# One level of Strassen's method for the up and down projections of a ConvFFN in a hybrid decoder layer

## The reference

```python
def conv_ffn(x, w_up, w_ffn_conv, b_ffn_conv, w_down):
    hid = jnp.einsum('bsd,df->bsf', x, w_up)          # 2048 -> 2 x 5632
    hid = causal_dwconv(hid, w_ffn_conv, b_ffn_conv)  # width 3, along the positions
    val, gate = hid[..., :D_FF], hid[..., D_FF:]
    return jnp.einsum('bsf,fd->bsd', jax.nn.silu(gate) * val, w_down)

def reference(x, ...):
    mix = hybrid_mixer(x, ...)     # input projection, short conv, mLSTM of 4 heads, output projection
    x = layer_norm(alpha * x + mix, ln1_g, ln1_b)
    return layer_norm(alpha * x + conv_ffn(x, ...), ln2_g, ln2_b)
```

## Time and profile before

| | us |
|---|---|
| three timed runs | 2342.16, 2343.01, 2343.11 |
| median | 2343.01 |
| profiled execution: span from first to last instruction | 2341.3 |
| around the span (median less span) | 1.7 |
| TensorE matmul busy, share of the span | 2302.4 (98%) |
| VectorE busy | 1099.8 (47%) |
| ScalarE busy | 588.2 (25%) |
| GpSimd busy | 103.9 (4%) |

### The profile page before, as it was taken

One profiled execution on the slowest core, in us unless ns is written; L12 is line 12 of the kernel. 1 busy time (PEld: TensorE's weight loads), 2 busy tenths in 40 slices (PEclk: granted clock), 3 DMA queues, 4 the chain that ended last, 5 costly groups with the idle time before them and its releaser, 6 DMA issues.

```text
span 2341.3 us, 24919 instructions
## 1 busy us (share of the span) xinstructions
PE 2302.4 (98%) x10248; PEld 1895.4 (81%) x10248; DVE 1099.8 (47%) x1130; ACT 588.2 (25%) x488; POOL 103.9 (4%) x62
## 2 busy tenths in 40 slices
PE   8999999999999998999999999999999999999996
PEld 7888888888888887888888888888888888888885
DVE  4354324433345569544444444544444444444448
ACT  4323222221133352222221212222221212222221
POOL 0000000000000039000000000000000000000003
PEclk9999999999999999999999999999999999999998
DMA  5322222232336532222222222222222222222231
GB/s 222 108 90 73 92 98 79 90 127 90 107 137 223 193 149 73 107 99 98 90 101 96 90 102 95 90 94 103 90 95 102 90 97 100 90 90 107 90 126 72
DMA packets 37151, 249.55 MB, mean 107 GB/s; under 512 B 4092, under 2 KB 4124, under 8 KB 7920
## 3 DMA queue, kind: packets, MB, share of 16 engines
...
HBM read 244.67 MB, written 4.19 MB: 106 GB/s over the span
## 4 chain that ended last, share of the span: by engine, by line
PE 95%; DVE 3%; DMA 1%; ACT 0%; issue 0%; POOL 0%; SPq 0%; DVEq 0%; ACTq 0%
PE ps L948 32%; PE ps L949 32%; PE ps L950 31%; DVE w_lo L567 1%; DMA raw<-w_mix 1%; DVE stream L886 0%; DVE stream L883 0%; PE ps L1148 0%; ACT w_hi L382 0%; DVE x_full L866 0%; DVE stream L816 0%; PE ps L1006 0%; POOL act_lo L354 0%; PE ps L978 0%; PE ps L977 0%
## 5 line engine op out<-in xcount | busy, mean ns | idle before, releaser
L948 PE MATMUL ps<-act_hi,w_hi 128*128 128x512 f32 (+1 forms) x2080 | 806.5, 388 | 10.0 <-DVE w_lo L567 6.2
L382 ACT ACTIVATE w_hi<-raw 128x2048 fp32r<-128x2048 f32 x220 | 421.8, 1917 | 1527.2 <-PE ps L950 1524.6
L949 PE MATMUL ps<-act_lo,w_hi 128*128 128x512 f32 (+1 forms) x2080 | 804.1, 387 | 0.0
L950 PE MATMUL ps<-act_hi,w_lo 128*128 128x512 f32 (+1 forms) x2080 | 804.0, 387 | 0.0
L567 DVE TENSOR_TENSOR w_lo<-raw,w_hi 128x2048 fp32r<-128x2048 f32 x219 | 512.9, 2342 | 358.3 <-ACT w_hi L382 358.3
L948 PEld LDWEIGHTS ps<-act_hi,w_hi 128*128 128x128 f32 x2080 | 392.1, 189 | 92.3 <-DVE w_lo L567 6.8
L950 PEld LDWEIGHTS ps<-act_hi,w_lo 128*128 128x128 f32 x2080 | 391.9, 188 | 79.1
L949 PEld LDWEIGHTS ps<-act_lo,w_hi 128*128 128x128 f32 x2080 | 392.1, 188 | 78.3
L949 PE MATMUL ps<-w_lo,h_hi 128*128 128x512 f32 x704 | 280.9, 399 | 0.0
L948 PE MATMUL ps<-w_hi,h_hi 128*128 128x512 f32 x704 | 277.4, 394 | 0.0
L950 PE MATMUL ps<-w_hi,h_lo 128*128 128x512 f32 x704 | 275.9, 392 | 0.0
...
## 6 DMA issues: line engine op xcount, KB each, us to landing
...
```

The source lines that it names most:

```text
L382: act.activation(w_hi[:, s % SPLIT, :], raw[:, s % RAW, :], ACT.Copy).then_inc(tile_hi, 1)
L948: pe.matmul(dst, a[0], b[0], start=first, stop=False)
L949: pe.matmul(dst, a[0], b[1], start=False, stop=False)
L950: return pe.matmul(dst, a[1], b[0], start=False, stop=last)
```

## The change

**The method.** Strassen's method (in Winograd's form) multiplies two matrices, each cut in 2 by 2 blocks, with 7 block products for 8, and pays with sums of blocks. For the up projection a *unit* is one tile of values and one of gates. Its weights are cut by value and gate and by the two halves of the 2048 inputs; the activations by the same halves and by the two halves of the 512 positions. A unit is 7 products of 8 blocks by 3 matmuls of 256 columns. The first pair of tiles stays as it was, in the window, and 43 units follow. For the down projection the 44 hidden tiles are taken in pairs, in 6 chunks (five of 4 pairs, one of 2); for each of the 7 products a pair is one *slot* of 12 matmuls of 512 columns.

**Sums.** The four weight sums of an up unit (128x1024 each) are done by POOL (`s1`, `s3`, `s2`, `s4` in this order), as are those of each down pair, except the four first sums of the first down chunk, which DVE does. The four activation sums of the up projection (128x2048) are done once by DVE; those of the down projection by POOL, four of 128x1024 for each chunk of 4 pairs. In place of 2048 the parts are 1024 wide: ACT and DVE make a high and a low part for each of the 7 products, from sums where the product needs one, into 3 buffers for up (two products ahead) and 5 for down (four ahead).

**Results.** Products are summed in PSUM where they can be; ACT copies four 128x256 results of a unit to SBUF (`hid`) and DVE adds the three others (`hid_add`). The first tap of the convolution is done by ACT, the two later ones by DVE, now from SBUF (`later_taps`). The finished hidden tile goes to DRAM (`h_dram`) and comes back in chunks, to be split there. The normalised rows go to DRAM too; POOL makes the scaled residual from them in 8 pieces of 128x1024, in units 4, 6, ... 18, and it comes back into `acc` before the down projection. The FFN part is written out instead of looped.

```diff
+ORDER = ("P1", "P2", "P6", "P5", "P7", "P3", "P4")
+NP = len(ORDER)
+N_UP = NP * GROUPS
+AHEAD = 2
+CHUNK_PAIRS = [4, 4, 4, 4, 4, 2]
+DOWN_SLOTS, DOWN_AHEAD = 5, 4
+BLOCK = {"P1": A11, "P2": A12, "P6": A11, "P5": AX, "P7": A21, "P3": AX, "P4": A22}
+TARGET = {"P1": (0, 0), "P2": (0, 0), "P6": (1, 0), "P5": (1, 1), "P7": (1, 1), "P3": (1, 0), "P4": (0, 1)}
...
+    def load_unit(m):
+        if m == 1:
+            sp.wait_ge(tile_lo, FF0 + 2)
+        elif m == 2:
+            sp.wait_ge(tile_done, FF0 + 2)
+        else:
+            sp.wait_ge(up_lo, NP * (m - 2))
+        sp.dma_start(unit[m % 2][:, A11:A12 + 1, :],
+                     w_up[2 * m].rearrange("p (b n) -> p b n", b=2)).then_inc(val_in[m % 2], 16)
+    def store_hidden(t):
+        sp.wait_ge(prod_ready, t + 1)
+        sp.dma_start(h_dram[t], prod[t % 2][:, :]).then_inc(h_out[t % 2], 16)
...
+    for m in range(1, GROUPS - 1):
+        store_hidden(m - 1)
+        load_unit(m + 2)
+        if m >= 3 and m % 2 and (m - 3) // 2 < PIECES:
+            load_residual((m - 3) // 2)
+        if m >= 4 and m % 2 == 0 and (m - 4) // 2 < PIECES:
+            store_residual((m - 4) // 2)
...
-    pool.wait_ge(x1_turned, KD)
-    pool.wait_ge(pool_step, 1)
-    for c in range(NS):
-        pool.tensor_tensor(rows[:, c, :], rows[:, c, :], ln_rows[:, 0, :], ALU.mult).then_inc(pool_step, 1)
-        pool.wait_ge(pool_step, c + 2)
-        pool.tensor_tensor(rows[:, c, :], rows[:, c, :], ln_rows[:, 1, :], ALU.add).then_inc(res_ready, 1)
+    for m in range(1, GROUPS + 1):
+        u = unit[m % 2]
+        pool.wait_ge(gate_in[m % 2], 16 * (loads_before(m) + 1))
+        pool.tensor_tensor(u[:, AX, :], u[:, A21, :], u[:, A22, :], ALU.add).then_inc(s1_up, 1)
+        pool.wait_ge(s1_up, m)
+        pool.wait_ge(val_in[m % 2], 16 * (loads_before(m) + 1))
+        pool.tensor_tensor(u[:, A21, :], u[:, A11, :], u[:, A21, :], ALU.subtract).then_inc(s3_up, 1)
+        pool.wait_ge(s3_up, m)
+        pool.wait_ge(up_lo, NP * (m - 1) + 1)
+        pool.tensor_tensor(u[:, A11, :], u[:, AX, :], u[:, A11, :], ALU.subtract).then_inc(s2_up, 1)
+        pool.wait_ge(s2_up, m)
+        pool.wait_ge(up_lo, NP * (m - 1) + 4)
+        pool.tensor_tensor(u[:, AX, :], u[:, A12, :], u[:, A11, :], ALU.subtract).then_inc(s4_up, 1)
+        r = (m - 4) // 2
+        if m >= 4 and m % 2 == 0 and r < PIECES:
+            if r % NS == 0:
+                pool.wait_ge(res_gb_in, 32 * (r // NS + 1))
+                pool.tensor_scalar(res_gb[:, :, :], res_gb[:, :, :], ALPHA, None, ALU.mult).then_inc(res_scaled, 1)
+                pool.wait_ge(res_scaled, r // NS + 1)
+            pool.wait_ge(res_z_in, 16 * (r + 1))
+            pool.tensor_tensor(res_z[:, :], res_z[:, :], res_gb[:, 0, :], ALU.mult).then_inc(res_mult, 1)
+            pool.wait_ge(res_mult, r + 1)
...
+    def down_s1(c, p):
+        n = sum(CHUNK_PAIRS[:c]) + p
+        if p == 0:
+            pool.wait_ge(da_in[A21], 16 * (c + 1))
+            pool.wait_ge(da22_in[c % 2], 16 * (c // 2 + 1))
+            pool.wait_ge(down_lo, SLOT0[c] - CHUNK_PAIRS[c - 1])
+        pool.tensor_tensor(dx[:, p, :], da21[:, p, :], da22[c % 2][:, p, :], ALU.add).then_inc(s1_down, 1)
...
+            for p in range(g):
+                down_s1(c, p)
+            for p in range(g):
+                down_s3(c, p)
+            down_t1(c, g)
+            down_t2(c, g)
+            for p in range(g):
+                down_s2(c, p)
+            down_t3(c, g)
+        for p in range(g):
+            down_s4(c, p)
+        down_t4(c, g)
+    pool.wait_ge(ln2_in, 32)
+    for f, c in enumerate(FIN):
...
+    def up_split(n):
+        m, i = unit_of(n)
+        if n >= 3:
+            act.wait_ge(up_done, n - 2)
+        else:
+            act.wait_ge(tile_done, FF0 + 2) if n else act.wait_ge(tile_lo, FF0 + 2)
+        if ORDER[i] in ("P1", "P2"):
+            act.wait_ge(val_in[m % 2], 16 * (loads_before(m) + 1))
+        elif ORDER[i] == "P4":
+            act.wait_ge(gate_in[m % 2], 16 * (loads_before(m) + 1))
+        else:
+            act.wait_ge({"P6": s2_up, "P5": s1_up, "P7": s3_up, "P3": s4_up}[ORDER[i]], m)
+        act.activation(slot_hi[(n + 2) % 3][:, :], unit[m % 2][:, BLOCK[ORDER[i]], :], ACT.Copy).then_inc(up_hi, 1)
...
+    def silu(m):
+        if m:
+            act.wait_ge(up_conv, 4 * m)
+        else:
+            act.wait_ge(ff_step, 6)
+        act.activation(yy[:, 1, :], yy[:, 1, :], ACT.Silu).then_inc(silu_done, 1)
...
+    def up_lo_part(n):
+        m, i = unit_of(n)
+        dve.wait_ge(up_hi, n + 1)
+        dve.tensor_tensor(slot_lo[(n + 2) % 3][:, :], unit[m % 2][:, BLOCK[ORDER[i]], :],
+                          slot_hi[(n + 2) % 3][:, :].bitcast(F32), ALU.subtract).then_inc(up_lo, 1)
...
+    def later_taps(m, t):
+        g = m - 1
+        c = (2 * m + t) * 4
+        dve.wait_ge(tap, 2 * g + t + 1)
+        for lag in (1, 2):
+            if lag == 2:
+                dve.wait_ge(up_conv, 4 * g + 2 * t + 1)
+            dve.scalar_tensor_tensor(yy[:, t, lag:SEQ], hid[g % 2][:, t, 0:SEQ - lag], fc[:, c + 2 - lag:c + 3 - lag],
+                                     yy[:, t, lag:SEQ], ALU.mult, ALU.add).then_inc(up_conv, 1)
...
+    for n in range(N_UP):
+        m, i = unit_of(n)
+        if n and ORDER[(n - 1) % NP] in ("P2", "P7", "P3"):
+            hid_add(n - 1)
+        if n + AHEAD < N_UP:
+            up_lo_part(n + AHEAD)
+        if n == 0:
+            gated(0)
+        if m > 1 and i in (1, 2):
+            later_taps(m - 1, i - 1)
+        if m > 1 and i == 4:
+            gated(m - 1)
...
+        for j in range(8):
+            last = mm3(ps[:, up_bank(m, i), 0:256], (hi[:, P * j:P * j + P], lo[:, P * j:P * j + P]),
+                       (xb[:, i, 0, j, :], xb[:, i, 1, j, :]), fresh and j == 0, j == 7, not fresh)
+        last.then_inc(up_done, 1)
...
+    def down_half(s, u):
+        c, i, p = DOWN[s]
+        what, g, k = ORDER[i], CHUNK_PAIRS[c], NP * c + i
+        fresh = what in ("P1", "P2", "P5") and p == 0
+        h, hi, lo = hc[k % 2], dslot_hi[s % DOWN_SLOTS], dslot_lo[s % DOWN_SLOTS]
+        for q in range(2):
+            last = mm3(ps[:, (0 if k % 2 else 4) + 2 * u + q, :],
+                       (h[:, 0, p, P * u:P * u + P], h[:, 1, p, P * u:P * u + P]),
+                       (hi[:, 512 * q:512 * q + 512], lo[:, 512 * q:512 * q + 512]), fresh, p == g - 1,
+                       what not in ("P1", "P2", "P5"))
+        return last
```

More of the change, by code:

```diff
@@ L63 @@
 FF0 = N_MIX + N_OUT
-GR0 = FF0 + 2
 CONV0 = MIX.index(("conv", 0, 0))
@@ L163, in build @@
[L163 to L173 removed]
+        ident = at("ident", [P, P], SM)
@@ new lines, in _ @@
+            hid_split(0, 0)
+            down_split(0)
+            hid_copy(N_UP - 1)
+            first_tap(GROUPS, 0)
+            first_tap(GROUPS, 1)
+            for s in range(1, DOWN_AHEAD):
+                down_split(s)
+                if s == 1:
+                    silu(GROUPS)
+            for s in range(N_DOWN):
+                c, i, p = DOWN[s]
+                if p == 0:
+                    k = NP * c + i + 1
+                    if k < NP * CHUNKS:
+                        hid_split(k // NP, k % NP)
+                if s + DOWN_AHEAD < N_DOWN:
+                    down_split(s + DOWN_AHEAD)
@@ new lines, in gated @@
+            def gated(m):
+                dve.wait_ge(silu_done, m + 1)
+                if m >= 2:
+                    dve.wait_ge(h_out[m % 2], 16 * (m // 2))
+                if m:
+                    dve.wait_ge(up_conv, 4 * m)
+                dve.tensor_tensor(prod[m % 2][:, :], yy[:, 1, :], yy[:, 0, :], ALU.mult).then_inc(prod_ready, 1)
+            dve.wait_ge(x1_full_act, sum(full_on_act(a) for a in range(2 * KD)))
+            dve.wait_ge(x1_full_dve, sum(not full_on_act(a) for a in range(2 * KD)))
@@ new lines, in down_product @@
+            def down_product(s):
+                c, i, p = DOWN[s]
+                what, g, k = ORDER[i], CHUNK_PAIRS[c], NP * c + i
+                pe.wait_ge(down_lo, s + 1)
+                if p == 0:
+                    pe.wait_ge(hc_lo, k + 1)
+                    if k == 0:
+                        pe.wait_ge(hid_dve, 3 * GROUPS)
+                    elif k == 1:
+                        pe.wait_ge(hid_act, 4 * GROUPS)
+                    else:
+                        pe.wait_ge(added, 2 * (k - 1))
+                for u in range(2):
+                    last = down_half(s, u)
+                last.then_inc(down_done, 1)
@@ new lines, in _ @@
+            for n in range(N_UP):
+                up_product(n)
+            end = N_DOWN - CHUNK_PAIRS[CHUNKS - 1]
+            for s in range(end):
+                down_product(s)
+            k = NP * CHUNKS - 1
+            pe.wait_ge(hc_lo, k + 1)
+            pe.wait_ge(added, 2 * (k - 1))
+            for u in range(2):
+                for s in range(end, N_DOWN):
+                    if u == 0:
+                        pe.wait_ge(down_lo, s + 1)
```

(2 more changed lines are left out.)

750 lines of the change are left out of this document (510 added, 240 removed).

## The result

The changed kernel takes 2510.29 us (median of 4 runs, 2508.93 to 2511.24) against 2343.06 (2342.16 to 2343.12) of the kernel before: a ratio of 1.0714, 95% interval 1.0699 to 1.0729. The forecast was 2567 with a range of 2385 to 2655, and slower with 0.90.

A forecast was written before the change was run, and what follows sets the result against it. The prediction took TensorE's matmul time to bound the kernel before. From 2343 us it added 171 (up), 34 (down), 14 (into the units) and 5 (tail) for 2567 us, range 2385 to 2655.

The forecast's parts named there:

- The mechanism: POOL's operations and DVE's two-input SBUF operations exclude each other and take turns; in up the port needs 21.1 us, TensorE 20.1.
- the signs: Trace marks of a right forecast, among them PE well below 90% busy and low parts of 1024 averaging 2 us or more.
- Rival A: The POOL-DVE lock seldom binds, TensorE stays the bound: about 2229 us, faster; chance 0.08.
- Rival B: The port is packed well, at its sum of 21.1 us per up unit: 2374 us, still slower; chance 0.17.
- Rival C: The clock falls in ordinary up units too, 77 us more from idle times of 1.7 and 2.3 us: 2644 us; chance 0.20.
- into the units: Between window and up units: first activation and weight sums delay the units' effective begin to 905 from 890.5, +14 us.
- The walk from x: One up unit's operations followed from the end of P5's low part: P3 starts at x + 12.55, 24.1 us in all.
- the clock's price: In eight up units with residual work, matmuls slow at granted clock 0.50: 2.2 us more each, 18 us.
- they count in full: In the up phase, the residual's POOL operations push sums and DVE operations behind them, adding their whole length: 48 us.
- costed at nothing: The DRAM round trips: no cost assumed; without cover at the first down chunk, its start gets up to 10 us longer.
- the port's sum: Lower bound of a down chunk of 4 pairs: POOL and DVE port operations add to 88 us, against TensorE's 78.
- The matmul saving: Up matmuls 936 to 865 us, down 493 to 431: together 133 us less, if TensorE never waits.

The follow-up runs named there:

- e2: Changed kernel with POOL's four up sums written to a block no product reads, products reading stored blocks (output differs): 2509.77 us, 1.0711 of the kernel before.
- e3: Changed kernel with the convolution's running sum moved to two free PSUM banks, so later taps and the gated product read PSUM; everything computed: 2365.29 us, 1.0097.
- e4: Changed kernel with POOL's arithmetic on the residual left out, loads and signals kept, so the output lacks the residual: 2460.57 us, 1.0503 of the kernel before.
- e6: e3 with eight of a down chunk's weight sums (the two s1 and s3) made on DVE in place of POOL: 2359.47 us, 1.0069 of the kernel before.
- e10: e3 with the down projection written as eight plain block products without sums, the up projection still by Strassen: 2325.51 us, 0.9928 of the kernel before.
- e12: e10 plus the residual's POOL work placed in the gaps of odd units, a unit later; everything computed: 2310.31 us, 0.9862 of the kernel before.

## Why the prediction was right, and where it was off

**The mechanism** held at every step that the runs could try. TensorE falls to 89%; its waits in the up phase end with `slot_lo` (152.6 of 155.5 us); `hid_add` stayed at 0.41 us; the granted clock dips in the units with residual work. Two of the signs were set too high: TensorE at 89% isn't well below 90%, and the mean low part is 1.71 and 1.95 us where 2 or more was expected. Rival A, that the lock seldom binds, is out: the units are 23.3 us long, and e2 and e3 show that it is POOL's work beside DVE's operations in SBUF that makes them so. Rival B, packed to its sum (21.1 us), lay 2.2 us below the measured unit. Rival C didn't come: from 1400 us on the granted clock is 1.00. But the idle times there, 0.93 and 1.58 us in each unit, are shorter than the 1.7 and 2.3 us that C was built on, so that much idle time in every unit was not tried.

**By terms, in us:**

| step | forecast | measured |
|---|---|---|
| an up unit | 24.2 | 23.3 |
| 43 units | 1041 | 1002 |
| residual and clock in the up phase | 66 | 50 (e4), 51 (trace) |
| up phase against before | +171 | +115 |
| down against before | +34 | +32 |
| into the units | +14 | +11 |
| tail | +5 | +10 |
| sum (of the unrounded rows) | +224 | +167 |

The measured up phase runs from 901.3 us (the start of the second unit, 924.6, less one unit) to 1951.9, so it is 1050.6 us long; that is 3 less than 1002.3 and 51.4, since the last unit takes 20 us.

**The up unit.** The walk from x (1448.00, the end of P5's low part) puts P3 at x + 12.55; its matmul stands at 1459.59, x + 11.6. The order of the operations was right to the last one. (The list of a unit's DVE operations ahead of the prediction also begins here, with P5's low part.) What was mis-sized are the steps at which the two engines take turns. From x on, the first tap and `s4` take 2.9 us (forecast 3.1), the second tap and `s1` 2.8 (3.1), P7's low part and `s3` 3.3 (3.55), the two taps 1.3 (1.55) and P3's low part 1.15: each of the first four is 0.2 to 0.3 shorter than the sum of the free durations. In the rows an operation begins before the one ahead of it has ended, as the tap at 1447.91 and `s4` at 1448.14; but a row also holds the wait for the other engine, so where in a turn the time is saved can't be read from them. The remaining part of the walk, from P3 to the next x, was forecast at 11.65 and is 11.7. This step is 39 of the 57 us by which the sum is too high.

**Residual and clock.** The full count of POOL's operations (48) and the clock's price (18) made 66. The excess over 41 units of 23.31 is 51 us in the trace, and e4 gives 49.7 for both together. No run takes the clock away alone, but the trace of the changed kernel divides the 51 us. Unit 8, which has residual work, and unit 22, which has none, each from its first matmul to the next unit's:

```profile
1076.59:1106.37 29.78, 23.14 (x171) 22.73 (x170) 24.58 (x16) 10.43 (x14) 17.27 (x7) 0.89 0.36 133
1442.27:1465.57 23.30, 20.79 (x171) 20.32 (x170) 20.84 (x16) 10.43 (x14) 11.25 (x5) 1.00 0.26 98
```

Unit 8 is 6.5 us longer. TensorE stands still for 6.6 us in it and for 2.5 in unit 22, so 4.1 us are waits; the other 2.35 are the same 168 matmuls (three more lie across the edges), which take longer at a granted clock of 0.89. Added up over the eight units with a piece, the waits are 33 us and the slower matmuls 18. The clock's price was right in sum (2.3 us a unit, though 1.1 to 4.6 in the single ones). The term that was too high is "they count in full": 48 us of POOL's work made 33 us of waiting.

**Down.** 527 us were forecast and 525 measured (1951.9 to 2476.6), but the agreement is luck: it has two errors in it that cancel. A chunk takes 91.7 us and not 96, and 5.5 of them 504 where 528 stood. The first chunk's faster `s1` and the last one's missing successor were to give 13 back and the start to take 12. Nothing came back at the end: the fifth chunk takes 86.0 us and the last half one 52.1, as much as one and a half of 91.7. And 20 us are lost at the entry: TensorE waits 2.4, 8.9, 1.7 and 7.1 us between 1955 and 2001. POOL had stood waiting 18.7 us for hidden rows on their way back from DRAM before it began these sums, a round trip that was costed at nothing; whether it or the order of DVE's queue is what holds up the entry was not tried. In the steady chunks the waits look like this in the trace of the changed kernel:

```profile
2246.76 0.77 PE L1393 MATMUL ps<-dslot_hi,hc 128*128 128x512 f32 x1 [5.51 <-DVE acc L1320]
```

```profile
2232.08 3.42 DVE L1290 TENSOR_TENSOR dslot_lo<-da22a,dslot_hi 128x1024 fp32r<-128x1024 f32 x1
2235.42 3.42 DVE L1297 TENSOR_TENSOR hc<-hb,hc 128x1024 fp32r<-128x1024 f32 x1
2238.77 3.42 DVE L1290 TENSOR_TENSOR dslot_lo<-da,dslot_hi 128x1024 fp32r<-128x1024 f32 x1
2242.11 1.21 DVE L1320 TENSOR_TENSOR acc<-acc,ps 128x1024 f32<-128x1024 f32 x1
2243.24 2.24 DVE L1290 TENSOR_TENSOR slot_lo<-da,slot_hi 128x1024 fp32r<-128x1024 f32 x1
2245.41 1.21 DVE L1320 TENSOR_TENSOR acc<-acc,ps 128x1024 f32<-128x1024 f32 x1
```

The two accumulations for which TensorE waits, at 2242.11 and 2245.41, read PSUM and take 1.21 us. They are late since three operations ahead of them in DVE's queue take 3.4 us each. The forecast's bound of 88 us (the port's sum) had the right size for another reason: DVE's own 57 us and 32 behind POOL. e6 excluded the sum, and e10 did without both parts.

The forecast priced a lower clock in the up units with residual work and put it at nothing in the down chunks. There it costs more. Of the 91.7 us of a steady chunk (the table under e6) 76.2 are 336 matmuls at 0.2267 and 11.0 are TensorE's four waits; the remaining 4.4 are matmuls that follow more slowly, at a granted clock of 0.94. In e10's chunk, without a wait, the granted clock is 1.00 and nothing remains. Over 5.5 chunks that makes 24 us at most (an estimate from this one chunk: some of it follows each wait at a full clock too, as in unit 22, where TensorE is busy for 20.8 us with matmuls that take 20.16 in e3).

**The tail** took 10 us more than before where one `finish` was put down at 5.

**The matmul saving** was right as a rate. With 0.120 us at 256 columns, e3's units run at 20.16 us, 867 in all for 936 before. It can be had only where nothing else is longer, which is what e12 shows. The Trainium skill's formula ("TensorE: Matmul & The Clock Gate", Back-to-back issue gap), which the page gives for an isolated matmul at full clock, makes 109.2 ns of it. No run here comes near it: at a TensorE busy for every microsecond, e3 shows 120 ns.
